# The first adaLN scale and shift of a diffusion backbone, computed in five column groups instead of four

## The reference

```python
def adaln_params(cond, w_mod, b_mod):
    m = jax.nn.silu(cond) @ w_mod + b_mod
    return m.reshape(cond.shape[0], 1, N_MOD, D_MODEL)

def modulated_norm(h, w, mod, i):
    return rmsnorm(h, w) * (1.0 + mod[:, :, 3 * i + 1]) + mod[:, :, 3 * i]

def swiglu(y, w_up, w_down):
    a, b = jnp.split(y @ w_up, 2, axis=-1)
    return (jax.nn.silu(a) * b) @ w_down
```

## Time and profile before

| what | value |
|---|---|
| median of three executions | 2116.18 us |
| the profiled execution, its own time | 2116.01 us |
| its span | 2114.2 us |
| PE busy in the span | 2105.1 us |
| DVE busy | 1442.1 us |
| ACT busy | 805.6 us |
| read from HBM | 312.16 MB, 148 GB/s over the span |
| mean granted clock of TensorE | 0.999 |

### The profile page before, as it was taken

The page is one execution under the profiler, slowest core; times in us unless marked ns, Lnnn a source line. Parts: engine busy times, 40 slices in busy tenths (PEclk is TensorE's granted clock), DMA queues, the critical chain, the costliest instruction groups (busy, mean ns, idle before and its releaser), DMA issues.

```text
span 2114.2 us, 26101 instructions
## 1 busy us (share of the span) xinstructions
PE 2105.1 (100%) x10451; PEld 1782.0 (84%) x10451; DVE 1442.1 (68%) x1992; ACT 805.6 (38%) x1196; POOL 0.2 (0%) x4
## 2 busy tenths in 40 slices
PE   9999999999999999999999999999999999999998
PEld 7888888888888888898888888888888898888887
DVE  5687877668588773577777777733335688778765
ACT  5322222456322322342222233222223665557654
POOL 0000000000000000000000000000000000000000
PEclk9999999999999999999999999999999999999999
DMA  8665555431555653355555545433333446765664
GB/s 272 210 178 164 171 166 157 139 90 41 159 155 159 189 150 93 92 148 173 174 168 164 170 137 148 142 93 100 92 100 107 131 122 198 207 210 154 188 190 145
DMA packets 461628, 319.65 MB, mean 151 GB/s; under 512 B 19758, under 2 KB 436934, under 8 KB 461126
## 3 DMA queue, kind: packets, MB, share of 16 engines
q1 hardware_dynamic: 439708, 244.95, 40.5%
q10 hardware_dynamic: 21800, 73.03, 10.6%
HBM read 312.16 MB, written 1.05 MB: 148 GB/s over the span
## 4 chain that ended last, share of the span: by engine, by line
PE 99%; DVE 0%; ACT 0%; issue 0%; DVEq 0%
PE bank L657 22%; PE bank L659 22%; PE bank L658 22%; PE bank L668 9%; PE bank L671 5%; PE bank L990 4%; PE bank L696 2%; PE bank L734 1%; PE bank L754 1%; PE bank L753 1%; PE bank L752 1%; PE bank L700 1%; PE bank L738 1%; PE bank L1034 0%; PE bank L1035 0%; PE bank L1036 0%
## 5 line engine op out<-in xcount | busy, mean ns | idle before, releaser
L1606 DVE TENSOR_TENSOR LO<-RAW,HI 128x1024 fp32r<-128x1024 f32 (+1 forms) x431 | 518.3, 1207 | 358.7 <-ACT HI L1132 358.4
L657 PE MATMUL bank<-Y,HI 128*128 128x512 f32 (+1 forms) x1416 | 550.1, 388 | 0.0
L659 PE MATMUL bank<-Y,LO 128*128 128x512 f32 (+1 forms) x1416 | 549.2, 388 | 0.0
L658 PE MATMUL bank<-Y,HI 128*128 128x512 f32 (+1 forms) x1416 | 549.2, 388 | 0.0
L1132 ACT ACTIVATE HI<-RAW 128x1024 fp32r<-128x1024 f32 (+1 forms) x431 | 438.2, 1039 | 216.3 <-DMA RAW<-in_w_in_dram 58.2
L658 PEld LDWEIGHTS bank<-Y,HI 128*128 128x128 f32 x1416 | 265.9, 188 | 54.9 <-issue 0.5
L657 PEld LDWEIGHTS bank<-Y,HI 128*128 128x128 f32 x1416 | 265.9, 188 | 54.8 <-issue 0.5
L659 PEld LDWEIGHTS bank<-Y,LO 128*128 128x128 f32 x1416 | 265.9, 188 | 54.6
L1617 DVE SCALAR_TENSOR_TENSOR MODACC<-MODRAW,SC,MODACC 128x1024 f32<-128x1024 f32 x224 | 277.2, 1279 | 2.4 <-DMA MODRAW<-in_w_mod_dram 2.0
L1331 ACT ACTIVATE TMP<-bank 128x512 f32<-128x512 f32 x66 | 39.4, 598 | 414.9 <-PE bank L659 334.2
L668 PE MATMUL bank<-Y,HI 128*128 128x512 f32 x720 | 181.0, 393 | 0.0
(11 more groups left out here) (293 smaller groups left out, 2537.6 us busy)
## 6 DMA issues: line engine op xcount, KB each, us to landing
RAW<-in_ffn_w_up_dram SPq DMA_DIRECT2D x170, 512.0 KB, 4.1
MODRAW<-in_w_mod_dram ACTq DMA_DIRECT2D x128, 512.0 KB, 4.3
RAW<-in_w_in_dram SPq DMA_DIRECT2D x128, 512.0 KB, 4.1
RAW<-in_ffn_w_down_dram SPq DMA_DIRECT2D x66, 512.0 KB, 3.6
RAW<-in_ffn_w_down_dram SPq DMA_DIRECT2D x24, 384.0 KB, 3.2
WM<-in_w_mod_dram SPq DMA_DIRECT2D x16, 512.0 KB, 9.1
RAW<-in_w_ret_out_dram SPq DMA_DIRECT2D x16, 512.0 KB, 4.4
RAW<-in_w_conv_out_dram SPq DMA_DIRECT2D x16, 512.0 KB, 3.7
```

What stands on the lines that cost most here:

```text
L657: mm(bank, hi, X[:, k, 0, cols], start=first, stop=False)
L658: mm(bank, hi, X[:, k, 1, cols], start=False, stop=False)
L659: return mm(bank, lo, X[:, k, 0, cols], start=False, stop=end)
L1606: V_.tensor_tensor(weights(v, 1), raw_weights(v), weights(v, 0).bitcast(F32), ALU.subtract).then_inc(lo_done, 1)
```

## The change

The five groups hold the blocks (0), (1), (2, 3), (4, 5), (6, 7). The tiles WM of groups 0 and 1 are 128 columns wide instead of 256, and each has its own four tiles, so there are 20 WM tiles in place of 16 with the same bytes; the w_up pieces of these two groups are one block deep, ten in place of eight. ADAROWS copies, `columns`, `mods0`, HIP and LOP follow the group's width. The semaphores' counts follow the number of groups.

On PE, `modulation(3)` moves ahead of the first `keep_clock(2)`, the second `keep_clock(2)` goes, and the third grows from 6 to 10. Groups 1 and 2 are laid between the products of blocks 0 and 1 in a new order. On DVE, `xn` is made in three portions: (0, 1) ahead of `mods0(0)`, (2, 3) behind block 0, (4, 5, 6, 7) behind block 1. The lines of the changed kernel are 4 to 18 higher than before for the same step.

```diff
+GROUPS = ((0,), (1,), (2, 3), (4, 5), (6, 7))
+LAST = len(GROUPS) - 1
+GROUP_OF = [g for g, ks in enumerate(GROUPS) for _ in ks]
...
-    WM = [place(f"WM{b}", [P, 4, GROUP], F32, zone + 4096 * b) for b in range(16)]
+    WM = [place(f"WM{4 * g + b}", [P, 4, P * len(ks)], F32, zone + 2048 * (4 * ks[0] + b * len(ks)))
+          for g, ks in enumerate(GROUPS) for b in range(4)]
...
-                        sp.dma_start(WM[b][:], w[:, k0:k0 + 4, sec * D + g * GROUP:sec * D + (g + 1) * GROUP]
-                                     ).then_inc(wm_landed[b], 16)
+                        at, n = sec * D + P * GROUPS[g][0], P * len(GROUPS[g])
+                        sp.dma_start(WM[b][:], w[:, k0:k0 + 4, at:at + n]).then_inc(wm_landed[b], 16)
...
-                    for g in range(4):
+                    for g in range(LAST + 1):
...
-                    modulation(0)
-                    modulation(1)
-                    modulation(2)
+                    for b in range(4):
+                        modulation(b)
                     drain_wait(pe, s.turn[7])
                     keep_clock(2, s.turn[7].bank)
-                    modulation(3)
-                    keep_clock(2, s.turn[7].bank)
                     columns(0)
-                    keep_clock(6, s.turn[7].bank)
+                    keep_clock(10, s.turn[7].bank)
                     four = (0, 2, 1, 3)
-                    for g in range(3):
-                        high_high(2 * g, four)
-                        high_low(2 * g, four)
-                        low_high(2 * g, four)
+                    high_high(0, four)
+                    for b in range(4, 8):
+                        modulation(b)
+                    high_low(0, four)
+                    columns(1)
+                    low_high(0, four)
+                    modulation(8)
+                    high_high(1, four)
+                    modulation(9)
+                    high_low(1, four)
+                    modulation(10)
+                    low_high(1, four)
+                    modulation(11)
+                    columns(2)
+                    for g in range(2, LAST):
+                        k = GROUPS[g][0]
+                        high_high(k, four)
+                        high_low(k, four)
+                        low_high(k, four)
                         for b in range(4 * g + 4, 4 * g + 8):
                             modulation(b)
-                        high_high(2 * g + 1, four)
+                        high_high(k + 1, four)
                         columns(g + 1)
-                        high_low(2 * g + 1, four)
-                        low_high(2 * g + 1, four)
+                        high_low(k + 1, four)
+                        low_high(k + 1, four)
...
-                    xn(0, 1, 2, 3, 4, 5)
-                    for g in range(4):
+                    xn(0, 1)
+                    for g, ks in enumerate(GROUPS):
                         mods0(g)
...
+                        y0_low(ks[0])
+                        pair_lo(0, g)
+                        pair_lo(1, g)
+                        xn(*((2, 3), (4, 5, 6, 7))[g])
```

More of the change, by code:

```diff
@@ L203, in plan @@
             s.rb_acc = p.acc(7)
-            s.rows = [p.acc(4 + g % 2) for g in range(4)]
-            s.cols_acc = [p.acc(7 - g % 2) for g in range(4)]
+            s.rows = [p.acc(4 + g % 2) for g in range(LAST + 1)]
+            s.cols_acc = [p.acc(7 - g % 2) for g in range(LAST + 1)]
             after.halves = []
@@ L410, in build @@
         drained = [sem(f"drained{b}") for b in range(8)]
-        wm_landed = [sem(f"wm_landed{b}") for b in range(16)]
+        wm_landed = [sem(f"wm_landed{b}") for b in range(4 * LAST + 4)]
         c_landed, vec_landed, keep_landed, lg_landed, mixc_landed = (
@@ L451, in build @@
         pair_hi_done, pair_lo_done = sem("pair_hi_done"), sem("pair_lo_done")
-        pair_landed = [[sem(f"pair_landed{i}{g}") for g in range(4)] for i in range(2)]
+        pair_landed = [[sem(f"pair_landed{i}{g}") for g in range(LAST + 1)] for i in range(2)]
         left_done, right_done, out_stored = sem("left_done"), sem("right_done"), sem("out_stored")
@@ L879, in columns @@
                         drain_wait(pe, s.rows[g])
-                        for m in range(2):
+                        for m in range(len(GROUPS[g])):
                             ins = mm(B[acc.bank][:, 4 * m:4 * m + 4], ADAROWS[:, g % 2, m * P:(m + 1) * P],
@@ L1275, in rows_out @@
                             act.wait_ge(cols_done, g - 1)
-                        A(ADAROWS[:, g % 2, :], B[acc.bank][:, 0:GROUP], ACT.Copy).then_inc(drained[acc.bank], 1)
+                        n = P * len(GROUPS[g])
+                        A(ADAROWS[:, g % 2, 0:n], B[acc.bank][:, 0:n], ACT.Copy).then_inc(drained[acc.bank], 1)
                     def pair_hi(i, g):
-                        ks = slice(2 * g, 2 * g + 2)
+                        ks = slice(GROUPS[g][0], GROUPS[g][-1] + 1)
                         act.wait_ge(pair_landed[i][g], 16)
                         ins = A(HIP[i][:, ks, :], RAWP[i][:, ks, :], ACT.Copy)
-                        if g < 3:
+                        if g < LAST:
                             ins.then_inc(pair_hi_done, 1)
@@ L1307, in _ @@
                         pair_hi(1, g)
-                        y0(2 * g, 2 * g + 1)
+                        y0(*GROUPS[g])
                     split_at[0] = 4
@@ L1867, in mods0 @@
                         drain_wait(dve, acc)
-                        w = VT[:, VT_NORM + 2 * g:VT_NORM + 2 * g + 2].rearrange("p (c m) -> p c m", c=1).broadcast_to([P, 2, 2])
-                        V_.scalar_tensor_tensor(AMUL[:, :, 2 * g:2 * g + 2], MODS[:, 1, :, 2 * g:2 * g + 2], 1.0, w,
+                        w = VT[:, VT_NORM + ks.start:VT_NORM + ks.stop].rearrange("p (c m) -> p c m", c=1).broadcast_to([P, 2, n])
+                        V_.scalar_tensor_tensor(AMUL[:, :, ks], MODS[:, 1, :, ks], 1.0, w,
                                                 ALU.add, ALU.mult).then_inc(mods0_done, 1)
                     def pair_lo(i, g):
-                        ks = slice(2 * g, 2 * g + 2)
-                        if g < 3:
+                        ks = slice(GROUPS[g][0], GROUPS[g][-1] + 1)
+                        if g < LAST:
                             dve.wait_ge(pair_hi_done, 2 * g + i + 1)
@@ L1925, in _ @@
                     drain_wait(dve, s.rb_acc)
-                    xn(0, 1, 2, 3, 4, 5)
-                    for g in range(4):
+                    xn(0, 1)
+                    for g, ks in enumerate(GROUPS):
                         mods0(g)
-                        y0_full(2 * g)
-                        if g:
+                        y0_full(ks[0])
+                        if len(ks) > 1:
                             pair_lo(0, g)
-                        y0_low(2 * g)
-                        if not g:
-                            pair_lo(0, g)
+                            y0_low(ks[0])
+                            pair_lo(1, g)
+                            y0_full(ks[1])
+                            y0_low(ks[1])
+                            continue
+                        y0_low(ks[0])
+                        pair_lo(0, g)
                         pair_lo(1, g)
-                        y0_full(2 * g + 1)
-                        y0_low(2 * g + 1)
-                        if not g:
-                            xn(6, 7)
+                        xn(*((2, 3), (4, 5, 6, 7))[g])
                     split_at[0] = 4
```

31 lines of the change are left out of this document (16 added, 15 removed).

## The result

| | before | after |
|---|---|---|
| median of ten executions | 2116.34 us (2116.07 to 2116.79) | 2121.15 us (2120.56 to 2122.89) |
| profiled execution, its own time | 2116.01 | 2121.07 |
| its span | 2114.2 | 2119.3 |

The ratio is 1.0024, with a 95% interval of 1.0015 to 1.0032. The changed kernel is slower by 0.24%, 4.8 us by the medians. The forecast was 2119.2, inside 0.2%; the rival in which TensorE's clock falls had 2121.2.

What follows compares the result with a forecast made beforehand. PE, gapless from 20.57 us, bounds the kernel. Start -1.8, modulations +1.0, columns +0.15, wait +0.2, bare chain +2.5 and switching 1.1 make +3.2, so 2119.2 us from a profiled 2116.01; range 2117.6 to 2121.3.

Steps and rivals of the forecast that it cites:

- the rival in which TensorE's clock falls: Behind the new pause ahead of high_high(2): clock falls to half, 2 us lost, 2121.2 us; chance 0.15.
- a clock of 0.5 near 30 us: Granted clock in the changed profile: reading 0.5 there would show the forecast wrong.
- What bounds the kernel: Whole run: PE runs without a gap from 20.57 us on, so no later wait swallows a delay or gain.
- Part 1: Up to the first product: it starts at 18.8 instead of 20.57 us, a gain of 1.8 us.
- Filler last: Ahead of the first product: ten keep_clock matmuls end at 18.8, behind Y at 18.2.
- The tiles of group 2: Ahead of modulation(11): no wait for tiles, since PE took the same bytes by 25.38 before.
- Part 2: From high_high(0) to high_high(2): the latter starts at 31.9 instead of 28.71 us, +3.2 us.
- the idle times predicted as 0.5 and 1.7: PE idle about 0.5 us ahead of columns(2) and 1.7 ahead of high_high(2), ended by ADAROWS and Y.
- the wait of 0.2 ahead of high_high(1): Behind modulation(8): it ends at 23.75, Y of block 1 is ready at 23.95, so PE waits 0.2 us.
- the 3.2 stays to the end: From high_high(2) on: both orders alike with no wait left, so the 3.2 us delay remains.
- granted clock 1.0 throughout: Whole changed profile: the clock stays at 1.0, also around the new pause.
- The rival's price: Behind the pause: some 4 us at half pace, judged from the run's start, 2 us lost; chance 0.15.

Runs made afterwards that it cites:

- e10: Changed kernel with keep_clock(2) ahead of columns(2), keep_clock(7) behind it, and keep_clock(7) instead of 10 ahead of high_high(0); 2119.01 us, ratio 1.0013.
- e2: Changed kernel with modulations 8 to 11 in one piece behind low_high(0), and columns(2) between high_high(1) and high_low(1); 2117.95 us, ratio 1.0009.
- e1: Changed kernel with its new pause filled: keep_clock(2) between modulation(11) and columns(2), keep_clock(7) behind columns(2); 2118.99 us, ratio 1.0012.
- e5: Changed kernel with only keep_clock(2) added ahead of columns(2), none behind; 2121.02 us, ratio 1.0021.
- e9: Changed kernel with only keep_clock(3) added directly behind columns(2); 2120.47 us, ratio 1.0019.
- e3: Kernel before, groups of two, with block 1 moved ahead of modulations 4 to 7, leaving the chain to high_high(2) bare; 2120.09 us, ratio 1.0016.
- e4: Kernel before with block 1 ahead of modulations 4 to 7, plus keep_clock(2) ahead of columns(1) and keep_clock(7) behind; 2118.68 us, ratio 1.0011.
- e11: Changed kernel with group 2's modulations placed by their tiles' landing, keep_clock 2 ahead of columns(2) and 3 behind low_high(1); 2117.92 us, ratio 1.0007.
- e6: Changed kernel with only keep_clock(7) added behind columns(2), none ahead; 2118.90 us, ratio 1.0014.
- e8: Kernel before with every w_mod tile loaded by two transfers of 128 columns, rows of 512 bytes instead of 1024; 2119.58 us, ratio 1.0015.

## Why the prediction was wrong

The measured 2121.15 lies within the stated range of 2117.6 to 2121.3, but 2.0 us above the forecast, and near the rival that had the chance of 0.15. By the prediction's own sign, a clock of 0.5 near 30 us, it was wrong. Its sum held up to high_high(2), in part by luck. Step by step:

- *What bounds the kernel* was right: a delay at the beginning stays. The trace shows it to the end, but for one wait of 0.4 near 1929 us, where it had PE without waits.
- *Part 1*: the first product at 18.8, measured 18.76, in an execution that began 0.29 late; the gain was 5.05 against 7.15 from the diagonal matmul, 2.1 us instead of 1.8. So the match of the two times is in part luck: the late start hides 0.3 us by which the sum was too long. Most of it is the filler, which took 2.24 from its start to the first product (16.52 to 18.76); the sum had put in 2.45, the row's whole length, though rows overlap. Modulations of 128 columns took 1.08 per group, predicted 1.10. Filler last: right, but by 0.3 and not 0.6 (e10).
- *The tiles of group 2*: "no cause of wait there" was right for this order. The reason given, that PE took these bytes by 25.38 before, does not hold: e2 shows the last of them landing at 26.4, still 2 us ahead of its use in the changed kernel.
- *Part 2*: the idle times predicted as 0.5 and 1.7 were 0.59 and 1.72; the wait of 0.2 ahead of high_high(1) came too (23.16 to 23.92 from modulation(8), where 0.57 was put for it alone); high_high(2) at 31.9 was 31.98, again with the late start in it: counted from the diagonal matmul the delay was 2.98, predicted 3.2. Without the clock's fall the kernel takes 2118.99 (e1), predicted 2119.2.
- **The failed step is the pause's price: "the 3.2 stays to the end" with "granted clock 1.0 throughout".** The rival with the clock was put at 0.15 and is what happened. The row on which I set it against the pause was the fall at the run's end, 2.8 us behind the last matmul, and the pause of 1.2 us that did nothing; and I took the columns between the two idle times for a protection. The changed kernel, e5 and e9 show both readings wrong: the clock fell to 0.50 behind 0.59 and 1.72 with the columns between, behind 1.72 in one piece, and behind 0.60 and 0.94 with matmuls between, which by the times happens in most executions. It cost 1.65 us. What the rows left open between 1.2 and 2.8 us I filled with the hope that the lower part of it was safe.
- The rival's price was 2 us, from the pace at the start of the run. That row can't carry it, for the granted clock reads 1.00 there too; why its records are slow no run here shows. Measured 1.65 in the profile; by the medians the filler gives back 2.2 in the changed kernel, 1.4 in e3 against e4. What makes 2.2 out of 1.65 is not settled; the changed kernel was timed beside other executions of before than e1, 0.12 apart. That the rival's 2121.2 meets 2121.15 is in part luck too: by the medians beside before, the order costs 2.5 (e1), not 3.0, and the clock 2.3, not 2.0.
- The page "TensorE: Matmul & The Clock Gate" of the Trainium skill, in the section on HAM oscillation, warns of waits between groups of matmuls. The trace agrees that such a wait can lower the clock: 0.50 behind 1.72 us of idle time in e5.

The change's idea itself cost more than it gave even without the clock: the start won 2.1 us, but half of the first group's modulations moved into the stream (1.1), and the new order left group 2's chain of 2.9 us bare.

Open: the wait at L834 (0.4 in the changed kernel, 0.8 in e2, none in any other run) was not traced to a cause. From high_high(4) to the end of the span e2 takes 0.7 us longer than before; the changed kernel takes 0.2 longer, no more than the spread of the other runs with five groups. Why the same pause lowers the clock in one execution and not in the next was not tried. e2 and e11 put products of block 1 into the chain's time; an order that fills it with work and still meets the tiles was not found.

## What to carry to other kernels

Ask of an idle time of PE two prices: its length, and what the clock may take behind it (1.65 us here, behind 1.5 to 2.3 us of idle time). The second part doesn't show in the pause, where the granted clock still reads 1.0, but in the matmuls after it. When a group is split to start earlier, look which work covered the next group's chain, and whether that cover still stands behind the last modulation. Here matmuls on an idle bank for 1.8 us of the pause (e6) kept the clock up, and three of them (e9) did not in most executions. Smaller groups also mean shorter rows and more transfers: check that the tiles still come in time (e2).

## What was not expected of the hardware

An idle time of 1.72 us (e5), and one of 0.60 followed by one of 0.94 (e9), lowered the granted clock to 0.50 for the matmuls behind it. One of 0.85 to 1.22 us at the start of every run here did not, nor did 1.44 us in e8, nor 1.30 and 0.88 in e2. It is not the same in each execution: e3 ran with idle times of 0.59 and 1.72 and a clock of 1.00 in its profile, while nine of its eleven executions were 0.5 to 1.5 us slower than that one and only one was faster. Transfers with rows of 512 bytes moved 297 to 302 GB/s, those with 1024 moved 350, with the DMA engines equally busy.
